# Relative bias tables of four heads from one matmul and one table load, bias added 256 columns at a time, lambda set up later

## What is computed

```
proj = h @ w_in                      # q, k, v, g_attn, glu, g_conv, gates
lam  = exp(sum(lq0*lq1)) - exp(sum(lq2*lq3)) + lambda_init
s    = q k^T * 64**-0.5              # 4 heads, 2 parts each, causal, 2048 tokens
s    = where(k_pos <= q_pos, s + rel_bias[t5_causal_bucket(q_pos, k_pos)], -1e30)
p    = softmax(s); p = p[part 0] - lam * p[part 1]
o    = rms_norm(p @ v, subln_w) * (1 - lambda_init) * silu(g_attn)
u    = a * sigmoid(b)                # GLU, then causal depthwise conv of width 31,
u    = silu(layer_norm(conv(u))) * silu(g_conv)
out  = (sigmoid(g1) * (o @ w_attn_proj) + sigmoid(g2) * (u @ w_conv_proj + b)) @ w_out
y    = layer_norm(2**0.25 * x + out)
```

## Time and profile before

| | us |
|---|---|
| median of 3 runs | 656.89 |
| lowest, highest | 656.51, 657.5 |
| the profiled execution | 657.15 |
| its span (slowest core, 3) | 655.6 |
| spans of the 8 cores | 652.0 to 655.6 |

### The profile page before, as it was taken

How to read it: one execution, slowest core, us unless ns; L and a number is a source line. 1 busy time by engine, 2 the same in 40 slices (tenths; PEclk the granted TensorE clock), 3 DMA queues, 4 the chain that set the end, 5 groups by cost and what they waited for, 6 DMA issues and landing times.

```text
span 655.6 us, 12783 instructions; the slowest of 8 cores (652.0 to 655.6 us)
## 1 busy us (share of the span) xinstructions
PE 609.7 (93%) x4384; PEld 317.4 (48%) x4384; DVE 299.6 (46%) x534; ACT 303.6 (46%) x461; POOL 210.2 (32%) x211
## 2 busy tenths in 40 slices
PE   4897999999999998999989988799999999999993
PEld 1342444455555555555545544344444444476771
DVE  1131621214655555536473848522248346544365
ACT  0221111367787768766885784222234233224341
POOL 8000000003171315222442456842222222227851
PEclk9997999999999999999999999899999999999998
DMA  8994283011401113111011817397025023112421
GB/s 110 168 160 64 72 139 66 12 47 48 84 19 37 50 37 53 44 48 45 1 36 36 129 32 128 58 163 168 0 65 161 32 65 116 77 33 96 131 97 64
DMA packets 29515, 49.06 MB, mean 75 GB/s; under 512 B 6251, under 2 KB 21004, under 8 KB 29068
## 3 DMA queue, kind: packets, MB, share of 16 engines
q0 software_dynamic: 9152, 19.93, 20.4%
q1 hardware_dynamic: 20300, 28.32, 14.8%
HBM read 50.13 MB, written 9.18 MB: 90 GB/s over the span
## 4 chain that ended last, share of the span: by engine, by line
PE 73%; DMA 7%; DVE 6%; issue 6%; POOL 4%; ACT 3%; DVEq 0%; SPq 0%; ACTq 0%; POOLq 0%
PE pd L580 19%; PE pd L1360 8%; PE pd L1244 8%; PE pd L1246 8%; PE pd L1033 7%; PE pd L1000 5%; DMA xT<-xt 4%; PE pd L1250 4%; PE pd L1248 4%; PE pd L757 4%; PE pd L1008 3%; DMA lamt<-lambda_qk 2%; ACT pT L1018 1%; DVE ycf L835 1%; PE pd L604 1%
## 5 line engine op out<-in xcount | busy, mean ns | idle before, releaser
L1018 ACT ACTIVATE pT<-pd 128x1024 bf16<-128x1024 f32 (+3 forms) x160 | 139.6, 901 | 41.5 <-PE pd L1008 20.2
L1033 PE MATMUL pd<-vaug,pT 128*128 128x130 bf16 x1088 | 88.6, 221 | 0.2 <-ACT osb L573 0.2
L1255 ACT ACTIVATE sg<-pd 128x512 f32<-128x512 f32 (+1 forms) x80 | 36.4, 507 | 99.0 <-PE pd L1250 96.4
L580 PE MATMUL pd<-xT,wh 128*128 128x512 bf16 x336 | 79.3, 379 | 2.5 <-DVE rstd L1076 0.7
L1033 PEld LDWEIGHTS pd<-vaug,pT 128*128 128x128 bf16 x1088 | 66.5, 98 | 26.2 <-issue 18.6
L1263 POOL TENSOR_TENSOR mergedT<-sg,sg 128x512 bf16<-128x512 f32 (+1 forms) x40 | 45.1, 1131 | 97.1 <-DVE sg L1260 95.3
L1244 PE MATMUL pd<-xT,wg 128*128 128x512 bf16 (+1 forms) x320 | 63.0, 340 | 1.4 <-ACT sg L1255 0.5
L1258 DVE TENSOR_TENSOR sg<-pd,sg 128x512 f32<-128x512 f32 (+1 forms) x40 | 23.3, 583 | 86.5 <-ACT sg L1255 86.2
L1246 PE MATMUL pd<-xT,wg 128*128 128x512 bf16 (+1 forms) x320 | 62.6, 339 | 0.0
L580 PE MATMUL pd<-xT,wab 128*128 128x512 bf16 x256 | 58.6, 392 | 4.0 <-DVE vaug L574 4.0
L1000 PE MATMUL pd<-qT,kT 64*128 64x512 bf16 (+3 forms) x320 | 56.8, 354 | 2.2 <-ACT pT L1018 2.2
(11 more groups left out here) (121 smaller groups left out, 801.9 us busy)
## 6 DMA issues: line engine op xcount, KB each, us to landing
xres<-x SPq DMA_DIRECT2D x16, 512.0 KB, 4.0
y<-hres SPq DMA_DIRECT2D x14, 512.0 KB, 2.7
u<-upad SPq DMA_DIRECT2D x192, 33.8 KB, 1.9
wg<-w_gate POOLq DMA_DIRECT2D x8, 512.0 KB, 9.7
wh<-w_head POOLq DMA_DIRECT2D x3, 768.0 KB, 8.2
u<-upad SPq DMA_DIRECT2D x64, 33.7 KB, 1.9
xT<-xt POOLq DMA_DIRECT2D x8, 256.0 KB, 15.8
wab<-w_ab POOLq DMA_DIRECT2D x4, 512.0 KB, 17.3
```

Source lines behind the costliest of these rows:

```text
L580: ins = e.matmul(ps[bank][:, :], w[:, c, c0:c0 + 128], xT[:, c, t * 512:(t + 1) * 512], start=(c == 0), stop=(c == KC - 1))
L1018: S.add("act", us=0.2 + 2 * ncol / 1230, fn=lambda e: e.activation(out=pT2[pi][:, :, 0:ncol], in_=pdv[:, :, 0:ncol], func=AF.Exp, scale=SC ...
L1033: ins = e.matmul(ps[bank][:, col:col + 130], pT2[pi][:, c, rr * 128 - c0:(rr + 1) * 128 - c0], vaug[:, j, h, :], start=(j == 0 and first), ...
L1255: S.add("act", lambda e, i=i, sg=sg: e.activation(out=sg[sl][:, 0:w], in_=ps[bk[i]][:, 0:w], func=AF.Sigmoid), writes=[("sg%d" % (i + 1), ...
```

## The change

Four things change.

- The bias rows of all heads come from one fp32 matmul: `lhsg` is one tile [33, 128] whose first four columns are the heads' biases (the rest zero), so partition h of the result holds head h. One copy, one subtraction on 4 partitions, one DMA of [4, 384] to DRAM.
- One DMA reads back the table of all heads, `btf` [128, 4, 256], with row step +1 instead of -1 shift: row p is shifted the other way. The order of the 128 keys is thereby reversed, and the weights of the bias matmul are the anti-diagonal matrix `anti` in place of the identity. `anti` is made by a memset on DVE, an affine select on POOL, and a cast on DVE.
- The blocks of distance 0 and 1 are now 256 neighbouring columns, so a key block whose two query blocks both lie in the tile takes one matmul of 256 columns for each part instead of two of 128. DVE scales `BT8` in 4 instructions of 256 columns instead of 8 of 128.
- Lambda and `subw8` are recorded later, at the start of `late_tables`.

```diff
+    S.add("dve", us=0.15, fn=lambda e: e.memset(antif[:, :], 1.0), writes=["antif"])
+    S.add("pool", us=0.5, fn=lambda e: e.affine_select(out=antif[:, :], in_=antif[:, :], compare_op=ALU.is_equal, fill=0.0,
+                                            base=-127, pattern=[[1, 128]], channel_multiplier=1),
+          reads=["antif"], writes=["antif"])
...
+    S.add("dve", us=0.2, fn=lambda e: e.tensor_copy(anti[:, :], antif[:, :]), reads=["antif"], writes=["anti"])
+    S.add("dve", us=0.15, fn=lambda e: e.memset(lhsg[:, :], 0.0), writes=["lhsg"])
...
     def setup():
         S.add("dve", us=0.15, fn=lambda e: e.memset(relb[32:33, :], 1.0), writes=["relb1"])
-        for h in range(4):
-            S.add("dve", us=0.2, fn=(lambda h=h: lambda e: e.tensor_copy(lhsg[h][:, :], relb[:, h:h + 1].to_broadcast([33, 128])))(),
-                  reads=["relb", "relb1"], writes=[("lhsg", h)])
+        S.add("dve", us=0.15, fn=lambda e: e.tensor_copy(lhsg[:, 0:4], relb[:, 0:4]), reads=["relb", "relb1"], writes=["lhsg"])
+
+    def lam_tables():
...
     def late_tables():
+        lam_tables()
...
+    def bias_rows():
+        gb = 2
+        S.add("pe", us=0.95, fn=lambda e: e.matmul(ps[gb][:, 0:384], lhsg[:, :], ohs[:, :], start=True, stop=True),
+              reads=["lhsg", "ohs"], banks=[B(gb)])
+        S.add("dve", us=0.17, fn=lambda e: e.tensor_copy(grow[0:4, 383:384], ps[gb][0:4, 382:383]), writes=["gfar"], banks=[B(gb)])
+        S.add("dve", us=0.6, fn=lambda e: e.tensor_scalar(out=grow[0:4, 0:383], in0=ps[gb][0:4, 0:383], scalar1=grow[0:4, 383:384], scalar2=None,
+                                                  op0=ALU.subtract), reads=["gfar"], writes=["grow"], banks=[B(gb)])
+        S.add("sp", lambda e: e.dma_start(out=gscr.ap()[:, :], in_=grow[0:4, :]), reads=["grow", "gfar"], writes=["gscr"], dma=3.0)
+        src = AP(gscr, 0, [[1, 128], [384, 4], [1, 256]])
+        S.add("sp", lambda e: e.dma_start(out=btf[:, :, :], in_=src), reads=["gscr"], writes=["btf"], dma=6.0)
...
-                for dist in range(2):
-                    qb_ = j + dist
-                    if qb_ < 4 * t or qb_ >= 4 * t + 4:
-                        continue
-                    off = (qb_ - 4 * t) * 128 - c0
-                    ins = e.matmul(ps[sb[c]][:, off:off + 128], ident[:, :], BT8[:, h, dist, :], start=False, stop=True,
-                                   skip_group_check=True)
+                if near is not None:
+                    lo, hi = near
+                    ins = e.matmul(ps[sb[c]][:, 0:hi - lo], anti[:, :], BT8[:, h, lo:hi], start=False, stop=True, skip_group_check=True)
```

More of the change, by code:

```diff
@@ L372, in build @@
     y_d = nc.dram_tensor("y", [T, D], F32, kind="ExternalOutput").ap()
-    gscr = nc.dram_tensor("gscr", [4 * 128, 384], F32)
+    gscr = nc.dram_tensor("gscr", [4, 384], F32)
     S = Sched(nc)
@@ L434, in build @@
     pT2 = [A.alloc("pT", [128, 2, 512], BF16) for _ in range(NPT)]
-    BT8 = A.alloc("BT8", [128, 4, 2, 128], BF16)
+    BT8 = A.alloc("BT8", [128, 4, 256], BF16)
+    anti = A.alloc("anti", [128, 128], BF16)
     epi_off = A.p
@@ L451, in build @@
     lamp = A.alloc("lamp", [128, 128], F32)
-    btf = [A.alloc("btf", [128, 128], F32) for _ in range(8)]
+    btf = A.alloc("btf", [128, 4, 256], F32)
+    antif = A.alloc("antif", [128, 128], F32)
     relb = A.alloc("relb", [33, 4], F32)
     ohs = A.alloc("ohs", [33, 384], F32)
-    lhsg = [A.alloc("lhsg", [33, 128], F32) for _ in range(4)]
-    grep = [A.alloc("grep", [128, 384], F32) for _ in range(4)]
+    lhsg = A.alloc("lhsg", [33, 128], F32)
+    grow = A.alloc("grow", [128, 384], F32)
     assert A.p <= ycf_off + 16384
     A.p = end_att
-    table_keys = ["lamt", "lamp0", "lamp1", "relb", "relb1", "ohs"] + [("lhsg", h) for h in range(4)] + \
-                 [("btf", i) for i in range(8)] + [("grep", i) for i in range(4)] + [("gfar", i) for i in range(4)]
+    table_keys = ["lamt", "lamp0", "lamp1", "relb", "relb1", "ohs", "lhsg", "btf", "grow", "gfar", "antif"]
     def load_wh(h):
@@ L612, in sink_v @@
               writes=[("v", n)], banks=[B(bank)])
-    bt8_pending = []
-    def flush_bt8():
-        while bt8_pending:
-            bt8_pending.pop(0)()
-    def g_step(h):
-        gb = 2 + h % 2
-        S.add("pe", us=0.95, fn=lambda e: e.matmul(ps[gb][:, 0:384], lhsg[h][:, :], ohs[:, :], start=True, stop=True),
-              reads=[("lhsg", h), "ohs"], banks=[B(gb)])
-        S.add("dve", us=0.17, fn=lambda e: e.tensor_copy(grep[h][:, 383:384], ps[gb][:, 382:383]), writes=[("gfar", h)], banks=[B(gb)])
-        S.add("dve", lambda e: e.tensor_scalar(out=grep[h][:, 0:383], in0=ps[gb][:, 0:383], scalar1=grep[h][:, 383:384], scalar2=None,
-                                               op0=ALU.subtract), reads=[("gfar", h)], writes=[("grep", h)], banks=[B(gb)])
-        S.add("sp", lambda e: e.dma_start(out=gscr.ap()[h * 128:(h + 1) * 128, :], in_=grep[h][:, :]),
-              reads=[("grep", h), ("gfar", h)], writes=[("gscr", h)], dma=5.0)
@@ L639, in build @@
+    def flush_bt8():
+        for h in range(4):
+            S.add("dve", us=0.35, fn=lambda e, h=h: e.tensor_scalar(out=BT8[:, h, :], in0=btf[:, h, :], scalar1=8.0, scalar2=None, op0=ALU.mult),
+                  reads=["btf"], writes=[("BT8", h)])
     thc = [0]
@@ L945, in build @@
         if t == 2:
-            for h in range(4):
-                g_step(h)
-            for h in range(4):
-                table_loads(h)
+            bias_rows()
     load_wab(2)
@@ L1173, in build @@
            ("th", [("th", i) for i in range(NTH)]), ("pT", [("pT", i) for i in range(NPT)]),
-           ("BT8", [("BT8", h, i) for h in range(4) for i in range(2)])]
+           ("BT8", [("BT8", h) for h in range(4)]), ("anti", ["anti"])]
     epi_keys = [(k, i) for k in ("o1", "o2", "od", "ssq", "rstd", "rs", "oab") for i in range(2)] + [("sga", i) for i in range(NSGA)] + \
```

14 lines of the change are left out of this document (3 added, 11 removed).

## The result

The changed kernel takes 650.94 us (median; 650.39 to 651.71) where the kernel before took 656.80 in the same runs: a ratio of 0.9909, 95% interval 0.9897 to 0.9921, or 5.9 us less. Run again on another chip, unedited, it gave 0.9910 (0.9894 to 0.9927). Executions in which the cores of one die ran at a lower mean clock than the others, and some per cent longer, are left out of every ratio here.

A forecast was written before the change was run, and what follows sets the result against it. PE, busy 93% of the span, was taken to bound the kernel. Terms -0.30 - 2.32 - 0.3 = -2.9 us against the profiled 657.15 gave 654.2, as median 654.0 us; 8 in 10 range 651.6 to 656.2.

The forecast's parts named there:

- the hole's cause and price: PE idle from 55.6 to 59.7 us: V block 8's cast waits behind `lamt`; 4.1 us, plus 2.89 us of lower clock.
- Part 1: Lambda recorded later on DVE: cast of V block 8 starts 0.62 us earlier; gain 0.3 us, between 0 and 0.62.
- the clock's rival: Behind PE's hole the clock falls for less time on all 8 cores: 1.2 or 2.89 us more gained; chance 0.08.
- The danger from `w4`: Making `w4` on DVE between the casts of V blocks 8 and 10: up to 1.0 us wait, not on the slowest core.
- Part 2: One fp32 table matmul instead of four on PE, and one border fewer: gain 2.32 us.
- Part 3: Attention bias matmuls of 256 columns instead of pairs of 128, in 48 groups: gain 0.3 us, between 0 and 1.1.
- Part 4: Small DVE and POOL instructions at the start, four scalings of `BT8` instead of eight: 0 us.
- Part 5: Scheduler's exchanged rows at five places of the attention stage: 0, with one place's price, 1.67 us, up or down.
- the case's own range: Whole kernel: 652.0 to 655.6 us, from the order's 1.67 us either way and the bounds of parts 1 and 3.
- an idle time in the attention stage differing by over 2 us: Sign of a wrong prediction: PE's idle time in the attention stage, expected near 19 us, differs by more than 2 us.
- a hole of less than 3 us: Sign of a wrong prediction: PE's hole behind the landing of `lamt` is under 3 us or gone.

The follow-up runs named there:

- lam_out: Changed kernel with the planned time of SP's small table loads raised from 3 to 14 us; ratio 0.9853 to the kernel before, 647.4 us.
- bef_out: Kernel before with only the planned time of SP's small table loads raised from 3 to 14 us; ratio 0.9890, 7.2 us faster.
- ord_t3: Changed kernel with the planner's old score group time for query tiles 0 to 2, the new one for tile 3 alone; ratio 0.9942 to the kernel before.
- f32_x4: Changed kernel with its one fp32 table matmul issued four times in a row; ratio 0.9941 to the kernel before.
- wide_only: Kernel before with only the bias of two blocks joined into one 256 column matmul, order kept; ratio 0.9996.
- order_old: Changed kernel with the planner's old time (4 x 0.07 us) for score groups with two near blocks; ratio 0.9933 to the kernel before.
- order_only: Kernel before with only the planner's new time (2 x 0.115 us) for score groups with two near blocks; ratio 0.9951, 3.2 us faster.

## Why the prediction was off

- **What bounds the kernel, and the hole's cause and price**: right. lam_out and bef_out show it, the latter with 7.2 us against 7.0, of which 5.9 to 6.5 lie ahead of the attention stage.
- **Part 1, lambda later, 0.3 us**: the cast came 0.58 us earlier behind the landing (0.62 predicted), so the step itself was right. Its price is not settled: 1.1 us by two runs, uncertainty 1.2, or 0.9 in the mean of the cores, uncertainty 0.8. That holds 0.3 and 0.62 as well as more. The profiled slowest core was like core 1 before, 5.30 us, as the clock's rival says; but its condition, that all 8 cores escape, did not hold: core 7 took 6.25 us and was not the slowest. The danger from `w4` was read rightly in kind. It was too small in size: 2.85 us of wait in ord_t3 against at most 1.0, and on the slowest core. In the changed kernel's own total it does not show.
- **Part 2, 2.32 us**: right in the traces, 2.2 us between the two chains. f32_x4 gives 2.1, with an uncertainty of 1.6. The convolution loads began at 69.06 instead of 81.03 us, and nothing followed from it.
- **Part 3, 0.3 us**: it fits, by wide_only.
- **Part 4, 0**: nothing speaks against it, but it was not run by itself.
- **Part 5, the order, 0 with 1.67 either way**: this is the term that failed. It gave 1.6 us by order_old, 1.0 of it in the stage, and 3.2 by order_only, 1.6 to 2.3 of it in the stage. I took it at nothing because the moved transposes need not be late, had followed the order at one border, and bounded the rest by one place's wait on DVE, 1.67 us, which holds the first measurement and not the second. The table of PE's waits shows that several waits of 0.4 to 1 us were exchanged at once: 7.1 us of waits went and 5.4 came.
- **The sum**: 1.1 + 2.1 + 0.3 + 1.6 = 5.1 us of the 5.9; with order_only's 3.2 for the order it is 6.7. The measured gain lies between them, within the uncertainty of the terms. The total missed the forecast by 3.1 us; the order accounts for 1.6 to 3.2 of that, and 0.8 may be lambda's.
- **The range**: the case's own range of 652.0 to 655.6 was said to take in the bounds of parts 1, 3 and 5. Added up, these give 654.0 - 0.32 - 0.8 - 1.67 = 651.2 and 654.0 + 0.3 + 0.3 + 1.67 = 656.3. That is wider than was stated, and 650.94 still lies 0.3 us below it.
- **The signs**: the sentence that an idle time in the attention stage differing by over 2 us would show the prediction wrong came true, with 2.4. By its words the sign of a hole of less than 3 us came true as well, with 2.67 us on core 1. It was a poor sign: the holes of one execution differ by 1.6 us from core to core, and their means, 3.7 and 3.0, differ by the 0.6 to 0.7 us that was forecast.

## What to carry to other kernels

When a scheduler places instructions by planned times, a changed number is a change of its own: price it by running the old kernel with the new number alone, and take as its bound the sum of PE's waits at all exchanged places, not one of them. A hole on PE costs its length and can cost slower matmuls behind it; before taking work from the path, look whether a planned transfer time that is too short (3 us planned, 14 to 17 measured) has put a wait in front of a cast that PE needs. Raising this number in the two lines that plan such loads gave more here (7.2 us) than the whole change (5.9), and both together 9.7.
